# A two-layer hybrid decoder step: bias table by row pitch, useless bf16 products in the bare rounds, top-k rounds and roots moved

## What is computed

```python
# indexer and top-k of the prompt (128 keys a query) and of a sample (256 of 4097 keys)
s = relu(einsum('bqhd,bld->bqhl', qi, ki) * 64**-0.5)
scores = einsum('bqhl,bqh->bql', s, wi) * 8**-0.5
idx = top_k(where(admissible, scores, -inf), topk)
# attention over the chosen keys, with a bias by distance
logits = einsum('bqkgd,bqjkd->bqkgj', qg, k_sel) * 64**-0.5
logits = logits + rel_bias[t5_bucket(q_pos - sel_pos)]
out = softmax(logits) @ v_sel
# recurrence
r, i = sigmoid(xb @ wa + ba), sigmoid(xb @ wx + bx)
log_a = -8.0 * r * softplus(-lam)
u = sqrt(-expm1(2.0 * log_a)) * (i * xc)
h[t] = exp(log_a[t]) * h[t-1] + u[t]
```

## Time and profile before

| | |
|---|---|
| median of 3 runs | 1351.44 us (1347.97 to 1353.28) |
| the profiled execution | 1351.15 us, span 1349.4 us, clock 0.963 |
| TensorE busy | 1256.8 us, 93% of the span |
| VectorE, ScalarE, POOL busy | 52%, 35%, 14% |
| slabs 0 to 9 | TensorE from 12.5 to 208 us |
| behind slab 9 up to the first count | 208 to 238.3 us |
| rounds 0 to 31 | 238 to 300 us |
| end of the sample attention, out_ab begins | 353.3 us |
| span of the rest | 996 us |

### The profile page before, as it was taken

One profiled execution on the slowest core, in us unless ns is written; L12 is line 12 of the kernel. 1 busy time (PEld: TensorE's weight loads), 2 busy tenths in 40 slices (PEclk: granted clock), 3 DMA queues, 4 the chain that ended last, 5 costly groups with the idle time before them and its releaser, 6 DMA issues.

```text
span 1349.4 us, 24444 instructions
## 1 busy us (share of the span) xinstructions
PE 1256.8 (93%) x9991; PEld 1213.2 (90%) x9993; DVE 702.3 (52%) x1279; ACT 470.2 (35%) x548; POOL 193.0 (14%) x285
## 2 busy tenths in 40 slices
PE   5998994795999999999999999999999999999995
PEld 5878993563899999999999999999899999999994
DVE  5267786767347555555522244644755555552323
ACT  5243235451224434343322234332543343432110
POOL 0111001106303111111100010030411111110000
PEclk9999997696799999999999999999999999999998
DMA  7143301002222222222222332112122222222211
GB/s 271 64 149 123 132 33 46 1 2 65 68 93 70 89 91 93 93 93 93 87 89 109 102 125 94 64 64 93 63 94 93 93 93 93 93 86 87 86 60 63
DMA packets 25992, 118.17 MB, mean 88 GB/s; under 512 B 7720, under 2 KB 9192, under 8 KB 13904
## 3 DMA queue, kind: packets, MB, share of 16 engines
q1 hardware_dynamic: 21184, 105.50, 22.4%
q0 software_dynamic: 2048, 10.54, 2.3%
q10 hardware_dynamic: 2704, 1.35, 0.4%
HBM read 113.91 MB, written 3.46 MB: 87 GB/s over the span
## 4 chain that ended last, share of the span: by engine, by line
PE 70%; DVE 2%; POOL 1%; ACT 1%; issue 0%; DVEq 0%
PE ps L814 22%; PE ps L815 22%; PE ps L817 22%; POOL xl L1802 1%; PE ps L831 1%; PE ps L950 1%; PE ps L947 1%; PE ps L948 1%; PE ps L1209 0%; DVE acc L1240 0%; DVE vtc L1765 0%; DVE yt L1794 0%; PE ps L1121 0%; DVE rstd L1244 0%; DVE xn L1244 0%
## 5 line engine op out<-in xcount | busy, mean ns | idle before, releaser
L814 PE MATMUL ps<-xh,w_h 128*128 128x260 f32 x1792 | 471.4, 284 | 7.9 <-POOL xl L1802 7.8
L815 PE MATMUL ps<-xl,w_h 128*128 128x260 f32 x1792 | 469.6, 283 | 0.0
L817 PE MATMUL ps<-xh,w_l 128*128 128x260 f32 x1792 | 361.0, 283 | 0.0
L814 PEld LDWEIGHTS ps<-xh,w_h 128*128 128x128 f32 x1792 | 339.4, 189 | 9.1 <-issue 7.6
L815 PEld LDWEIGHTS ps<-xl,w_h 128*128 128x128 f32 x1792 | 338.8, 189 | 0.1
L1233 DVE TENSOR_TENSOR w_l<-w_raw,w_h 128x2048 fp32r<-128x2048 f32 (+1 forms) x94 | 211.6, 2251 | 166.4 <-ACT w_h L503 166.2
L817 PEld LDWEIGHTS ps<-xh,w_l 128*128 128x128 f32 x1792 | 277.1, 189 | 0.0
L815 PE MATMUL ps<-hl,w_h 128*128 128x260 f32 x704 | 183.9, 282 | 0.0
L503 ACT ACTIVATE w_h<-w_raw 128x2048 fp32r<-128x2048 f32 (+1 forms) x50 | 92.3, 1846 | 262.2 <-PE ps L817 242.4
L814 PE MATMUL ps<-hh,w_h 128*128 128x260 f32 x704 | 183.4, 282 | 0.0
L947 PE MATMUL ps<-xh,w_h 128*128 128x260 f32 x448 | 128.9, 309 | 14.1 <-DVE xl L1253 12.5
(11 more groups left out here) (298 smaller groups left out, 1406.3 us busy)
## 6 DMA issues: line engine op xcount, KB each, us to landing
w_raw<-in_wstream SPq DMA_DIRECT2D x86, 1024.0 KB, 4.8
w_raw<-in_wstream SPq DMA_DIRECT2D x8, 768.0 KB, 4.2
res<-in_x_t SPq DMA_DIRECT2D x4, 520.0 KB, 8.3
out_y<-yt SPq DMA_DIRECT2D x8, 260.0 KB, 2.2
tabf<-bias_by_distance SPq DMA_DIRECT2D x1, 2048.0 KB
wm<-in_sgu_w ACTq DMA_DIRECT2D x1, 512.0 KB, 3.6
sb_b<-in_sgu_b ACTq DMA_DIRECT2D x1, 512.0 KB, 4.2
out_f<-ost SPq DMA_DIRECT2D x2, 198.0 KB, 4.6
```

The lines of the kernel that those rows point to most:

```text
L814: pe.matmul(out[h], wh, hi[h], start=(first and k == 0), stop=False)
L815: pe.matmul(out[h], wh, lo[h], start=False, stop=False)
L817: ins = pe.matmul(out[h], wl, hi[h], start=False, stop=(last and k == nk - 1))
```

## The change

- The product `table`, its reversed identity, `tabf` and ScalarE's copies are gone. SP writes the bias by distance to DRAM eight times, at a pitch of 640 (two DMAs behind slab 3's load), and reads `tab` in sixteen DMAs of 8 partitions each behind slab 5's load, with a pitch of 639 from one copy to the next, so that each partition is shifted by one. VectorE waits for them before the first logits. Pool no longer waits for the table, nor for the gate products before `identb`.
- `decay_constants` and its two ScalarE steps move from slab 5 to slab 1.
- The values are turned beside slab 9's step 12 and copied before `evac_b(9)`.
- All 48 top-k rounds are in the slabs; `page_columns` is split, the first half in slab 6, the second behind slab 9.
- TensorE does three bf16 products of 128 x 512 without use behind each count of rounds 0 to 7 (`warm`), and waits for the last top-k before round 0.
- In `p_work` the pair of the next round comes first.
- The recurrence's shares (VectorE) and second exponentials (`rates`, ScalarE) are in rounds 9 to 12, the root in round 17.

```diff
-            sp.wait_ge(f_ev, 2)
-            sp.dma_start(scratch.ap(), fneg[:]).then_inc(d_scr, 16)
             for s in range(2, 10):
                 sp.wait_ge(w_hi, s - 1)
                 sp.wait_ge(w_lo, s - 1)
                 load(s, s % 2)
-                if s == 2:
-                    sp.wait_ge(d_scr, 16)
-                    sp.dma_start(tabf[:], bass.AP(scratch.ap().tensor, 0, [[1, P], [640, 8], [1, SEQ]])).then_inc(d_scr, 16)
+                if s == 3:
+                    sp.wait_ge(f_ev, 2)
+                    for h in range(2):
+                        sp.dma_start(bass.AP(scratch.ap().tensor, h * 8 * 640, [[2 * 8 * 640, 4], [640, 8], [1, 640]]),
+                                     fneg[4 * h:4 * h + 4, :].rearrange("p (a c) -> p a c", a=1).broadcast_to((4, 8, 640)))\
+                            .then_inc(d_scr, 16)
+                if s == 5:
+                    sp.wait_ge(d_scr, 32)
+                    for r in range(0, P, 8):
+                        sp.dma_start(tab[r:r + 8], bass.AP(scratch.ap().tensor, P - 1 - r,
+                                                           [[639, 8], [8 * 640, 8], [1, SEQ]])).then_inc(d_tabs, 16)
...
-            def table(m):
-                act.wait_ge(tab_mm, m + 1)
-                act.activation(tab[:, m, :], ps[:, 4 + m % 2, :], ACT.Copy).then_inc(tab_ev, 1)
...
+                if g == 1:
                     act.wait_ge(sp_z, 1)
...
-                    if g in (1, 2) and step % 4 == 3:
-                        table(4 * (g - 1) + step // 4)
...
-            for j in range(4):
+
+            def rates(j):
+
                 act.activation(rr[:, j, :], rr[:, j, :], ACT.Exp, scale=lamt[:, 7, j:j + 1]).then_inc(ex_done, 1)
-            act.wait_ge(e_done, 4)
-            act.activation(th[:], th[:], ACT.Sqrt).then_inc(sqrt_done, 1)
+
+            def roots():
+
+                act.wait_ge(e_done, 4)
+                act.activation(th[:], th[:], ACT.Sqrt).then_inc(sqrt_done, 1)
...
+                if 9 <= rnd < 13:
+                    rates(rnd - 9)
+                if rnd == 17:
+                    roots()
...
-            def table(m):
-
-                pe.wait_ge(d_scr, 32)
-                pe.wait_ge(d_flip, 16)
-                if m >= 2:
-                    pe.wait_ge(tab_ev, m - 1)
-                pe.matmul(ps[:, 4 + m % 2, :], flip[:], tabf[:, head_of(m), :], start=True, stop=True).then_inc(tab_mm, 1)
-
...
+                if g == 9 and step == 12:
+                    turn_values()
+
+            def turn_values():
+
+                pe.wait_ge(ev_a, NUNITS_I - 1)
+                for n in range(NCH):
+                    ins = pe.transpose(ps[:, 4, n * P:(n + 1) * P], vt[:, n * P:(n + 1) * P], ident[:])
+                ins.then_inc(vn_tr, 1)
...
-            for n in range(NCH):
-                ins = pe.transpose(ps[:, 2, n * P:(n + 1) * P], vt[:, n * P:(n + 1) * P], ident[:])
-            ins.then_inc(vn_tr, 1)
...
             def p_work(rnd):
 
+                for i in heads(rnd + 1):
+                    if i % 2 == 0:
+                        p_pair(i // 2)
                 for i in heads(rnd - 1):
                     p_turn(i)
                 for i in heads(rnd - 2):
@@ -1038,12 +1040,17 @@
                 for blk in range(NCH - 1):
                     if rnd == LAST[blk] + 4:
                         p_out(blk)
-                for i in heads(rnd + 1):
-                    if i % 2 == 0:
-                        p_pair(i // 2)
-
+
+            def warm():
+
+                for n in range(3):
+                    pe.matmul(ps[:, 3, :], sameb[:], pickb[NCH - 1][:], start=True, stop=True)
+
+            pe.wait_ge(topk_done, 3)
             for rnd in range(32):
                 count(rnd)
+                if rnd < 8:
+                    warm()
                 p_work(rnd)
...
+
+            def page_terms_out():
+
                 dve.tensor_copy(ptab[:, NK:NK + 1], col("chunk", 0))
                 dve.tensor_copy(ptab[:, NK + 1:NK + 3], pgc[:, :, 0])
                 tt(ptab[:, NK + 3:NK + 4], pgc[:, 0, 1:2], pgc[:, 0, 0:1], ALU.subtract)
                 ch.link(tt(pgf[:, 0, 0:1], pgc[:, 1, 1:2], pgc[:, 1, 0:1], ALU.subtract))
                 ts(ptab[:, NK + 4:NK + 5], pgf[:, 0, 0:1], float(-P), None, ALU.add).then_inc(page_terms, 1)
 
-            rounds = {4: (0, 0, 3), 5: (4, 4, 2), 6: (4, 4, 2), 7: (4, 4, 2), 8: (0, 0, 0), 9: (4, 5, 0)}
+            rounds = {4: (0, 0, 3), 5: (4, 6, 2), 6: (4, 5, 2), 7: (4, 6, 3), 8: (0, 0, 2), 9: (4, 3, 0)}
             q = 0
...
-                if g == 5:
+                if g == 1:
                     decay_constants()
...
+                if g == 9:
+                    dve.wait_ge(vn_tr, 1)
+                    dve.wait_ge(d_kvi, 48)
+                    dve.tensor_copy(vn[:].rearrange("p n c -> p (n c)"), ps[:, 4, :]).then_inc(vn_ev, 1)
                 evac_b(g)
+                if g == 6:
+                    page_columns()
                 if g >= 4:
...
-            dve.wait_ge(vn_tr, 1)
-            dve.wait_ge(d_kvi, 48)
-            dve.tensor_copy(vn[:].rearrange("p n c -> p (n c)"), ps[:, 2, :]).then_inc(vn_ev, 1)
-            page_columns()
-            topk_rounds(q, 3 * ROUNDS - q)
+            page_terms_out()
+            assert q == 3 * ROUNDS
...
                 blk, m, nk = i // 8, i % 8, P * (i // 8 + 1)
+                if i == 0:
+                    dve.wait_ge(d_tabs, 16 * 16)
                 dve.wait_ge(qk_done, i + 1)
...
             for rnd in range(32):
                 compare(rnd)
-                if 2 <= rnd < 6:
-                    rg_share(rnd - 2)
+                if 9 <= rnd < 13:
+                    rg_share(rnd - 9)
...
-            pool.wait_ge(tab_ev, 8)
             pool.memset(pick[0][:], 0.0).then_inc(pstep, 1)
...
-            pool.wait_ge(gate_mm, 8)
             pool.wait_ge(causal, NCH)
...
```

More of the change, by code:

```diff
@@ L88, in build_step @@
     (wstream, x_t, vec, rg_w, h0, conv0, ffn0, pages, page2, cache_kv, cache_i, rel, rel4, sgu_w, sgu_b,
-     sgu_w0, sgu_b0, c_ident, c_flip, c_dist, c_blocks, c_pick, c_slots) = ins
+     sgu_w0, sgu_b0, c_ident, c_dist, c_blocks, c_pick, c_slots) = ins
     y_o, k_o, v_o, ki_o, h_o, c_o, cv_o, f_o = outs
@@ L175, in build_step @@
         fneg = at("fneg", [8, 640], F32, o_gg + 2560)
-        flip = at("flip", [P, P], F32, o_gg + 5120)
         relt = at("relt", [32, 8], F32, o_gg + 5632)
         blocks = at("blocks", [P, 2, P], F32, o_gg + 5696)
-        tabf = at("tabf", [P, 8, SEQ], F32, o_ik)
         rr, ii, th = (at(n, [P, 4, T], F32, o_xn + 8320 * i) for i, n in enumerate(("rr", "ii", "th")))
@@ L275, in build_step @@
         ps = ctx.enter_context(nc.psum_tensor("ps", [P, 8, 512], F32))
-        scratch = nc.dram_tensor("bias_by_distance", (8, 640), F32)
+        scratch = nc.dram_tensor("bias_by_distance", (8, 8, 640), F32)
         by_token = nc.dram_tensor("scores_by_token", (DEC, NT * P), F32)
@@ L292, in build_step @@
         d_st, hst_done, ap_mm = sem("d_st"), sem("hst_done"), sem("ap_mm")
-        d_flip = sem("d_flip")
+        d_tabs = sem("bias_table")
         d_wax, d_rgs, d_pt = sem("d_wax"), sem("d_rgs"), sem("d_pt")
@@ L298, in build_step @@
         setup_v = sem("setup_v")
-        f_mm, f_ev, tab_mm, tab_ev = sem("f_mm"), sem("f_ev"), sem("tab_mm"), sem("tab_ev")
+        f_mm, f_ev = sem("f_mm"), sem("f_ev")
         wi_tr, wi_nat, idx_mm, relu_done, score_acc, causal, topk_done = (
@@ L353, in grp @@
             return ps[:, 4 * parity + 2 * tile:4 * parity + 2 * tile + 2, 0:HT]
-        def head_of(m):
-            return m // 2 + 4 * (m % 2)
         FILL = {"in_ab": 0, "out_ab": 1, "up0": 2, "in_c": 3, "out_c": 4, "up1": 5}
@@ L414, in _ @@
             load(1, 1)
-            for dst, src, done in ((flip, c_flip, d_flip), (pt, pages, d_pt), (pg2, page2, d_const),
+            for dst, src, done in ((pt, pages, d_pt), (pg2, page2, d_const),
                                    (blocks, c_blocks, d_const), (picks, c_pick, d_const), (h0s, h0, d_rgs)):
                 sp.dma_start(dst[:], src).then_inc(done, 16)
-            sp.wait_ge(f_ev, 2)
-            sp.dma_start(scratch.ap(), fneg[:]).then_inc(d_scr, 16)
             for s in range(2, 10):
@@ L839, in bias_products @@
                 pe.matmul(ps[0:8, 5, 0:128], relt[:], dist[:, 512:640], start=True, stop=True).then_inc(f_mm, 1)
-            def table(m):
-                pe.wait_ge(d_scr, 32)
-                pe.wait_ge(d_flip, 16)
-                if m >= 2:
-                    pe.wait_ge(tab_ev, m - 1)
-                pe.matmul(ps[:, 4 + m % 2, :], flip[:], tabf[:, head_of(m), :], start=True, stop=True).then_inc(tab_mm, 1)
             def turn_weights():
-                pe.wait_ge(tab_ev, 8)
                 pe.wait_ge(d_c, 16)
@@ L1950, in shape_constants @@
                             2.0 * P * (p % 16)], 1).astype(np.float32)
```

(6 more changed lines are left out.)

## The result

The changed kernel takes 1331.14 us (median of 4 runs, 1329.05 to 1332.56) beside 1351.23 for the kernel before: ratio 0.9853, 95% interval 0.9833 to 0.9874. The forecast was 1322.0 us with a range of 1316 to 1330: the direction is right, some 9 us of the gain are missing, and the time lies 1.1 us beyond the range. The profiled execution took 1329.75 us, its span is 1328.0 us, 21.4 less than before.

What follows compares the result with a forecast made beforehand. The prediction took a full TensorE queue as the bound, with a hole before the rounds whose start VectorE's list sets. Its terms sum to -29.1 us, 1351.15 - 29.1 = 1322.0 us, range 1316 to 1330.

Steps and rivals of the forecast that it cites:

- Table, decay, the slabs: Slabs: table by DMA -6.8 us, decay inputs in slab 1 -5.6, turned values +0.45, top-k rounds +1.9.
- Rival 3: Slabs: VectorE falls behind, page columns at 5 us, a 6 us wait before slab 9; about 1328 us, chance 0.12.
- rival 4: Slabs: the table rows clog the DMA rings and load 6 lands late; about 1360 us at 25 GB/s, chance 0.01.
- Early round 0: After slab 9: count(0) comes 10.6 us behind its end instead of 30.3; -19.7 us, ends -21 and -17.5.
- Bare rounds: Rounds 0 to 8, count(0) to compare(9), 9.85 us before: -0.2 us, ends -1.8 and +3.5.
- Rival 1: Bare rounds and rounds 9 to 14: the useless products don't hold 2.4 GHz; about 1326 us, chance 0.20.
- Rounds 9 to 14: First rounds with heads: 12.0 us at full clock instead of 13.2 at half; -1.2 us, ends -4 and +1.
- the ring: Two-head rounds, not in the prediction: next pair waits for logits' bank, turns for that pair, exponentials for turns, logits for exponentials.
- Pairs first: From round 15 on: next round's pairs first take away 0 to 2.4 us of TensorE's waits; -1.2 us taken.
- Later roots: Round 17: root and two table loads, 4.5 us on ScalarE, leave TensorE standing; +3.2 us, ends 0 and +5.
- rival 2: Around round 17: the roots hide and pairs-first gives its full 2.4 us; about 1317.5 us, chance 0.20.

Runs made afterwards that it cites:

- w11: The changed kernel with the useless products in rounds 0 to 10 instead of 0 to 7; 1324.88 us, ratio 0.9817.
- w11_last: The changed kernel with useless products in rounds 0 to 10 and the pairs at the end of a round's products; 1323.61 us, ratio 0.9804.
- w11_mixed: The changed kernel with useless products in rounds 0 to 10, pairs last in rounds 0 to 15 and first from round 16 on; 1322.12 us.
- w11_mixed_fill: w11_mixed with twelve useless products of 512 columns in round 18, ahead of the turn behind the roots; 1320.13 us, ratio 0.9771.
- w11_roots_last: The changed kernel with useless products in rounds 0 to 10, roots ahead of round 9, pairs last in a round; 1322.79 us.
- pairs_last: The changed kernel with the pairs at the end of a round's products again, as in the kernel before; 1326.30 us, ratio 0.9821.
- nowarm: The changed kernel without the useless products; 1331.62 us, ratio 0.9863.
- late0: The changed kernel with top-k rounds, turned values, page columns and Pool's wait where the kernel before had them; 1348.38 us, ratio 0.9985.
- before_warm: The kernel before with three useless products in each of rounds 0 to 10; 1347.6 us, ratio 0.9981.
- fill_tail: w11_mixed_fill with useless products in TensorE's pauses behind round 31 too; 1319.37 us, ratio 0.9765.

## Why the forecast was wrong, step by step

*Table, decay, the slabs: right.* The query eviction of slab 4 starts 7.2 us earlier (6.8 forecast for the table), slab 9 ends 10.9 us earlier (10.05 forecast for table, decay, turned values and top-k), and the wait for eviction A before slab 9 is 1.27 us (1.9). Rival 3, VectorE behind in the slabs, did not come; nor did rival 4: SP's next load went out at 97.76 and no slab waited for it.

*Early round 0: right.* Count(0) starts 10.3 us behind slab 9's end (10.6); what ended last was the sigmoid (the 0.79 in its row), not the sorted scores, though these are close: VectorE waited 3.05 us for them.

*Bare rounds: right, at little.* 9.09 us from count(0) to compare(9), 9.85 before: -0.8 for -0.2. Rival 1 fell as it was priced: the clock was at 1.00 from 207 to 218 us, through the pauses of up to 0.40 us between the groups of products. The Trainium skill, "TensorE: Matmul & The Clock Gate", section "A second HAM failure mode: psum-queue depth-cycling", has short pauses between groups of bf16 products of 512 columns make the clock swing; this trace does not agree, with each us from 208 to 217 busy at 0.60 to 0.89.

*Rounds 9 to 14: the first step that failed.* I took it that the clock which the useless products hold would be there for the heads. The sum's own place for the fault is plain: "Bare rounds 0 to 8" and "Rounds 9 to 14" stood in two terms, the useless products end in round 7, and nothing looked at what TensorE has from there to the first dense round (0.59 busy from 217 to 218 us). 12.0 us were forecast, 15.0 came. With the clock held (w11) it was 12.4, so the condition was wrong. That 12.4 is so near to 12.0 is in part luck: with the clock held and the pairs last (w11_last) the same rounds, with the same shares in them, take 10.6 us. My list of VectorE's work in a round was too long (1.95 us, where compare(9), (10) and (11) of w11_last stand 1.8 and 1.7 apart), and the ring, which I had not seen, made up for it with 1.8.

*Pairs first: the wrong sign.* I looked for what the order could take away, in rounds from 15 on, where TensorE's waits are 4%, and not at what it puts behind a wait in the rounds with two heads. What was left out: a product that is moved forward takes its waits along, and the turns now stand behind them. The runs show +6.9 us on the kernel before (ratio 1.0051) in place of -1.2, and 2.6 us at full clock up to compare(16). The clock, with this order, comes back some 20 us later (252 against 233 in the changed kernel, 280 against 262 in the kernel before). Only the late rounds, one head each, have the gain that I looked for (1.1 us).

*Later roots: the hole right in kind, its clock left out.* In the changed kernel TensorE stands 1.29 us for the root, less than my 3.2, since half-clock products fill most of ScalarE's 4.5 us: half of rival 2, but at no profit, for it is the slow clock that hides the roots. In w11 it stands 3.35, as forecast, and then loses the clock for 6 us; I had put that loss in as a bound (1.7 us) and left it out of the sum. Filling the hole gave 2.0 us by the medians of w11_mixed and w11_mixed_fill, whose intervals overlap.

*The balance, in spans:* forecast -29.1, measured -21.4. Up to compare(9) 31.6 us were gained where the terms have 29.95 (10.05 + 19.7 + 0.2), 1.7 more. Rounds 9 to 14 miss 3.0. From compare(15) to out_ab the changed kernel takes 100.5 us, the kernel before 91.9: +8.6 for +2.0, so 6.6 more. 3.0 + 6.6 - 1.7 is 7.9, and 0.1 came back behind it. The other 1.4 us to the median are the profiled execution, which was at the fast end of its runs. The stretch behind round 31 (54.8 us, before 56.8) gave nothing away here, but in w11 (56.3) and w11_roots_last (57.6) it took back 1.5 to 3 us of what the rounds had won.

*The range* was too narrow for two reasons. Rival 1 priced a lost clock at 4 us, by the rounds up to 14 alone, because in the kernel before it came back there; that it could come back later was in no case. And the pairs first had the bounds 0 and 2.4 us of gain, with no case in which they cost. Either fault mended brings the time into the range: 1324.9 in w11, 1326.3 in pairs_last.

## What to carry over

A clock that is held by filler is worth what it meets at its end: carry the filler to the first dense work, and look for the next hole (here one of 3.35 us, behind which it was lost again). Before products are moved to the head of a queue, follow what each of them waits for, and count the ring it closes separately for rounds with one and with two items. Where a granted clock stands in a term, write down when it falls and when it comes back as terms of their own.

## What was unexpected of the hardware

- A full queue did not bring the clock back: 33 us at 0.50 with TensorE busy at 0.99 in the changed kernel (219 to 252), 26 in nowarm, 22 in late0 (238 to 260), 14 in the kernel before (248 to 262). The records count a matmul that waits in the queue as busy (the four pair products take 1.35 us in w11 and 0.70 in w11_last at the same clock), so part of this is idle time that the profile does not show; with the pairs first there is more of it. That this is the cause is argued, not shown.
- Useless bf16 products of 512 columns, three a round, held 1.00 at 60 to 89% busy, and raised it from 0.50 in three rounds (before_warm). One by one between products over 32 rows they did not raise it in 14 us (fill_tail), and in one row, behind that, they did within 3.
- A stand of TensorE of 3.35 us was followed by 6 us of half clock (w11), one of 2.91 us in pairs_last by a fall too (0.55 from 246 to 252 us).
- VectorE's small update takes 0.58 and 0.73 us beside Pool's products in rounds 1 and 2, as in the earlier trace rows, and 0.16 in round 9.
